# The last 32 tokens of a 16384-expert layer taken out of its dense products and gathered instead

## The reference, cut to what matters

```python
s = einsum('chpd,hpnd->chpn', (xb @ wq), keys)      # 8 heads, two halves, 128 keys each
sv, si = top_k(s, 16)                               # per half
cand, cidx = sums of the pairs, si0 * 128 + si1
top_s, sel = top_k(cand, 16); eidx = cidx[sel]      # 16 experts of 16384 per head and token
g = softmax(top_s)
act = gelu(einsum('chkd,cd->chk', u_tab[eidx], xb))
return einsum('chk,chkd->cd', g * act, v_tab[eidx])
```

## Time and profile before

| | |
|---|---|
| median of 3 runs | 3477.69 us (3469.15 to 3482.21) |
| profiled execution | 3476.73 us |
| its span, first to last instruction | 3474.9 us |
| mean granted TensorE clock | 0.942 |
| busy: PE, PEld | 3244.1 us (93%), 2621.2 us (75%) |
| busy: DVE, ACT, POOL | 1652.2 us (48%), 988.6 us (28%), 1323.9 us (38%) |
| first Gelu of the U pass, first and last matmul start of the V pass | 458.4, 1267.3 and 1963.6 us |

### The profile page before, as it was taken

The page is one execution under the profiler, slowest core; times in us unless marked ns, Lnnn a source line. Parts: engine busy times, 40 slices in busy tenths (PEclk is TensorE's granted clock), DMA queues, the critical chain, the costliest instruction groups (busy, mean ns, idle before and its releaser), DMA issues. The chain is left out here.

```text
span 3474.9 us, 40090 instructions
## 1 busy us (share of the span) xinstructions
PE 3244.1 (93%) x15270; PEld 2621.2 (75%) x15270; DVE 1652.2 (48%) x3968; ACT 988.6 (28%) x1534; POOL 1323.9 (38%) x637
## 2 busy tenths in 40 slices
PE   8696899999999999999999899899988899889998
PEld 7454687878787788888888578688867789768886
DVE  6764259989898623333333354433023055433311
ACT  2333233333333321111111212222212256422221
POOL 3101243434333345555555334344423145324442
PEclk9767899999999999999999999899989879989999
DMA  3001145546465665555555222222322000112231
GB/s 115 11 1 55 62 123 161 180 144 194 148 191 149 194 215 194 194 194 194 194 194 194 73 84 80 79 97 95 105 85 97 24 1 1 49 56 97 97 110 66
DMA packets 179844, 399.22 MB, mean 115 GB/s; under 512 B 13332, under 2 KB 80788, under 8 KB 175300
## 3 DMA queue, kind: packets, MB, share of 16 engines
q1 hardware_dynamic: 179508, 394.55, 35.3%
q10 hardware_dynamic: 144, 2.10, 0.2%
HBM read 327.39 MB, written 69.21 MB: 114 GB/s over the span
## 5 line engine op out<-in xcount | busy, mean ns | idle before, releaser
L239 POOL TENSOR_TENSOR peer_wt_lo<-peer_wt,peer_wt_hi 128x1024 fp32r<-128x1024 f32 x272 | 713.4, 2623 | 1095.8 <-ACT peer_wt_hi L232 1095.8
L239 POOL TENSOR_TENSOR ffn_w_lo<-ffn_w,ffn_w_hi 128x1024 fp32r<-128x1024 f32 (+1 forms) x120 | 314.6, 2622 | 453.7 <-ACT ffn_w_hi L232 453.7
L232 ACT ACTIVATE peer_wt_hi<-peer_wt 128x1024 fp32r<-128x1024 f32 x272 | 287.9, 1059 | 615.9 <-PE peer_psum L251 604.2
L249 PE MATMUL peer_psum<-xn_hi,peer_wt_hi 128*128 128x512 f32 x1088 | 435.3, 400 | 11.3 <-DVEq L447 11.1
L251 PE MATMUL peer_psum<-xn_hi,peer_wt_lo 128*128 128x512 f32 x1088 | 427.9, 393 | 0.0
L250 PE MATMUL peer_psum<-xn_lo,peer_wt_hi 128*128 128x512 f32 x1088 | 427.4, 393 | 0.0
L249 PE MATMUL peer_psum<-peer_w_hi,peer_wt_hi 128*128 128x512 f32 x1024 | 398.5, 389 | 0.7 <-ACT peer_act_out L1230 0.7
L250 PE MATMUL peer_psum<-peer_w_lo,peer_wt_hi 128*128 128x512 f32 x1024 | 398.3, 389 | 0.0
L251 PE MATMUL peer_psum<-peer_w_hi,peer_wt_lo 128*128 128x512 f32 x1024 | 398.3, 389 | 0.0
L1255 DVE TENSOR_SCALAR peer_first_hot<-peer_iota,idx,gate 128x128 f16<-128x128 f16 x1024 | 330.6, 362 | 0.0
L249 PE MATMUL ffn_psum<-ffn_hn_hi,ffn_w_hi 128*128 128x512 f32 x704 | 279.3, 397 | 20.2 <-DVEq L447 20.0
(11 more groups left out here) (354 smaller groups left out, 5860.3 us busy)
## 6 DMA issues: line engine op xcount, KB each, us to landing
peer_wt<-in_peer_uT SPq DMA_DIRECT2D x128, 512.0 KB, 4.3
peer_wt<-in_peer_v SPq DMA_DIRECT2D x128, 512.0 KB, 3.7
ffn_w<-in_f_w_gu SPq DMA_DIRECT2D x88, 512.0 KB, 3.6
peer_act<-peer_act_out SPq DMA_DIRECT2D x128, 256.0 KB, 4.6
peer_gate<-peer_gates_out SPq DMA_DIRECT2D x16, 2048.0 KB, 10.4
peer_gates<-peer_gate SPq DMA_DIRECT2D x32, 1024.0 KB, 5.0
peer_act_in<-peer_act SPq DMA_DIRECT2D x128, 256.0 KB, 2.6
ffn_w<-in_f_w_down SPq DMA_DIRECT2D x32, 704.0 KB, 4.0
```

The lines of the kernel that those rows point to most:

```text
L232: act.activation(self.hi[:, n % self.pairs, 0:c], self.buf[:, n % self.n, 0:c], ACT.Copy).then_inc(self.rounded, 1)
L239: pool.tensor_tensor(self.lo[:, n % self.pairs, 0:c], self.buf[:, n % self.n, 0:c], self.hi[:, n % self.pairs, 0:c].bitcast(F32), ALU.subt ...
L249: pe.matmul(out, w[0], x[0], start=start, stop=False)
```

## The change: what it does, and the diff

The last 32 tokens (`GT`) leave both dense passes, so that each dense matmul has 480 columns (`DTOK`) instead of 512; the stored activations and gates shrink with it. The gate blocks of these tokens (four of the 64, at tiles 110 to 113) are not made.

For the 32 tokens the expert rows are gathered. The 128 partitions hold four parts (`GRP`) of 32 tokens; each part takes 32 (`STEPS`) of a token's 128 experts. At step s POOL fetches by indirect DMA one row of 1024 floats for each partition (512 KB), into a ring of six (`ROWS`). For the U table DVE multiplies it with the token's row and sums it to one number (`first`); ACT applies Gelu to the 128x32 numbers; DVE makes the shares; for the V table DVE adds the row times its share to `acc` (`second_of`). `fold` adds the four parts on PE, in eight small matmuls beside the last V tile, which waits for `summed`.

The token rows are transposed on PE at tile 97 (`token_rows`, 16 float32 matmuls) and copied by ACT; at tile 100 SP spreads numbers, gates and rows over the partitions. Fetches 0 to 7 are issued by POOL between its last eight U splits, the others after them. DVE does the first eight steps ahead of the V pass, steps 8 to 31 at even tiles n = 0 to 46, and the V steps at even n = 52 to 114. POOL no longer splits the V tiles: DVE does (`split_to(dve, ...)`), between `L1359` and `L338` of the tile. A copy of the U table in row order is added to the inputs.

```diff
@@ -949,6 +955,12 @@
 HB = 8
 QB = 32
 QUAD = 4
+GT = 32
+DTOK = SEQ - GT
+GRP = P // GT
+STEPS = PH * TOPK // GRP
+ROWS = 6
+EARLY = 8

 def peer(kit, io):
...
+        share = at("shares", 48896, [P, STEPS])
+        fold = at("fold", 49152, [P, GT])
+        row = at("row_here", 50720, [P, D])
+
         shared = nc.sbuf_base
         room = st.sb("room", [P, 2 * CT * SEQ * 2])
         mix = Split(nc.alloc_sbuf_tensor_at("peer_mix_hi", [P, 2 * CT, SEQ], F32R, offset=shared),
                     nc.alloc_sbuf_tensor_at("peer_mix_lo", [P, 2 * CT, SEQ], F32R, offset=shared + 2 * CT * SEQ * 4))
+        G = nc.alloc_sbuf_tensor_at("peer_gathered", [P, ROWS, D], F32, offset=shared)
+        acc = nc.alloc_sbuf_tensor_at("peer_gather_sum", [P, D], F32, offset=shared + ROWS * D * 4)
...
         O1 = nc.alloc_sbuf_tensor_at("peer_first_hot", [P, 2, 2, HB, NK], F16, offset=io["mixT_at"] + 2 * HB * NK * 2)
         iota = st.sb("iota", [P, NK], F16)
...
@@ -1061,7 +1092,17 @@
 
         def block_at(c):
             j, b = divmod(c - TURN - 1, SLOTS)
-            return j * NB + b if 0 <= j < ST and b < NB else None
+            return j * NB + b if 0 <= j < ST and 0 <= b < NB and j * NB + b < DTOK // HB else None
+
+        def first_step(n):
+
+            return EARLY + n // 2 if n % 2 == 0 and EARLY + n // 2 < STEPS else None
+
+        SHARES = 2 * (STEPS - EARLY) + 3
+
+        def second_step(n):
+            s, odd = divmod(n - SHARES - 1, 2)
+            return s if not odd and 0 <= s < STEPS else None
 
         with nc.Block() as block:
...
-                        sp.dma_start(a_dram[n * P:(n + 1) * P, :], Ao[:, n % AS, :]).then_inc(a_stored[n % AS], 16)
+                        sp.dma_start(a_dram[n * P:(n + 1) * P, :], Ao[:, n % AS, 0:DTOK]).then_inc(a_stored[n % AS], 16)
+                    if c == SLOTS * (ST - 1) + TURN + 3:
+                        sp.wait_ge(experts_known, 2)
+                        for g in range(GRP):
+                            sp.dma_start(mine[g * GT:(g + 1) * GT, :, :],
+                                         chosen[P - GT:P, :, g * STEPS:(g + 1) * STEPS]).then_inc(spread, 16)
+                        sp.wait_ge(rows_copied, 1)
+                        for g in range(GRP):
+                            sp.dma_start(row[g * GT:(g + 1) * GT, :], rows[P - GT:P, :]).then_inc(spread, 16)
                     b = block_at(c - 1)
                     if b is not None and (b + 1) % (QB // HB) == 0:
                         s = b // (QB // HB)
...
@@ -1117,7 +1166,22 @@
 
             @block.gpsimd
             def _(pool):
-                lin.ring.split_all(pool)
+                def fetch(s, table):
+                    if s >= ROWS:
+                        pool.wait_ge(row_used, s - ROWS + 1)
+                    pool.indirect_dma_start(G[:, s % ROWS, :], None, table,
+                                            bass.IndirectOffsetOnAxis(mine[:, 0, s % STEPS:s % STEPS + 1], 0))\
+                        .then_inc(fetched[s % ROWS], 16)
+
+                lin.ring.split_to(pool, U0 + NK - EARLY)
+                pool.wait_ge(spread, 32 * GRP)
+                for i in range(2):
+                    pool.wait_ge(g_stored[i], 16 * len(range(i, DTOK // QB, 2)))
+                for s in range(EARLY):
+                    fetch(s, t["peer_u"])
+                    lin.ring.split_to(pool, U0 + NK - EARLY + s + 1)
+                for s in range(EARLY, 2 * STEPS):
+                    fetch(s, t["peer_u"] if s < STEPS else t["peer_v"])
 
             @block.tensor
...
+
+                def token_rows():
+
+                    last = slice(SEQ - P, SEQ)
+                    pe.wait_ge(s_copied, 4 * ST)
+                    for k in range(DT):
+                        to = ps[:, 4 + k // 4, (k % 4) * P:(k % 4 + 1) * P]
+                        pe.matmul(to, xn.hi[:, k, last].bitcast(F32), kit.ident[:, :], start=True, stop=False)
+                        mm = pe.matmul(to, xn.lo[:, k, last].bitcast(F32), kit.ident[:, :], start=False, stop=True)
+                    mm.then_inc(rows_turned, 1)
...
+                            token_rows()
                     if block_at(c) is not None:
                         gate_block(block_at(c))
...
-                        mm = product(pe, ps[:, c % 2, :], (whi[:, p], wlo[:, p]), xn.pair(slice(None), k),
-                                     k == 0, k == DT - 1)
+                        mm = product(pe, ps[:, c % 2, 0:DTOK], (whi[:, p], wlo[:, p]),
+                                     xn.pair(slice(None), k, slice(0, DTOK)), k == 0, k == DT - 1)
                     mm.then_inc(lin.done, 1)
 
                 pe.wait_ge(gelued, NK)
-                pe.wait_ge(gcopied, SEQ // 4)
+                pe.wait_ge(gcopied, DTOK // 4)
+                pe.wait_ge(rows_copied, 1)
                 pe.wait_ge(taken, 4 * ST)
                 for n in range(NK):
                     whi, wlo = lin.ring.take(pe, V0 + n)
                     pe.wait_ge(w_lo, n + 1)
+                    if n == NK - 1:
+                        pe.wait_ge(summed, 1)
                     for d in range(DT):
                         p = slice(d * P, (d + 1) * P)
-                        mm = product(pe, ps[:, d, :], (whi[:, p], wlo[:, p]), Ws.pair(slice(None), n % WS),
-                                     n == 0, n == NK - 1)
+                        mm = product(pe, ps[:, d, 0:DTOK], (whi[:, p], wlo[:, p]),
+                                     Ws.pair(slice(None), n % WS, slice(0, DTOK)), n == 0, n == NK - 1)
                         if n == NK - 1:
-                            mm.then_inc(odone, 1)
+                            pe.matmul(ps[:, d, DTOK:SEQ], acc[:, p], fold[:, :], start=True, stop=True).then_inc(odone, 1)
...
+                        act.activation(rows[:, :].rearrange("p (i n) -> p i n", i=2), ps[:, 4:6, :], ACT.Copy)\
+                            .then_inc(rows_copied, 1)
                     if c >= AS:
                         act.wait_ge(a_stored[c % AS], 16 * (c // AS))
                     act.wait_ge(lin.done, U0 + c + 1)
-                    act.activation(Ao[:, c % AS, :], ps[:, c % 2, :], ACT.Gelu).then_inc(gelued, 1)
+                    act.activation(Ao[:, c % AS, 0:DTOK], ps[:, c % 2, 0:DTOK], ACT.Gelu).then_inc(gelued, 1)
+                lin.ring.round_to(act, V0 + SHARES)
+                act.wait_ge(dotted, 1)
+                act.activation(dots[:, :], dots[:, :], ACT.Gelu).then_inc(dots_gelued, 1)
                 lin.ring.round_to(act, V0 + NK)
 
...
+                    if j == ST - 1:
+                        dve.scalar_tensor_tensor(out=chosen[:, 0, :], in0=three[:, 0, :], scalar=float(NK), in1=three[:, 1, :],
+                                                 op0=ALU.mult, op1=ALU.add).then_inc(experts_known, 1)
+                        dve.tensor_copy(chosen[:, 1, :].bitcast(F32), three[:, 2, :]).then_inc(experts_known, 1)
                     for b in range(NB):
-                        hots(j * NB + b)
+                        if j * NB + b < DTOK // HB:
+                            hots(j * NB + b)
+                dve.wait_ge(experts_known, 2)
+                dve.wait_ge(turned, ST)
+                own.link(dve.tensor_tensor(fold[:, :], kit.ident[:, 0:GT], kit.ident[:, GT:2 * GT], ALU.add))
+                for g in range(2, GRP):
+                    own.link(dve.tensor_tensor(fold[:, :], fold[:, :], kit.ident[:, g * GT:(g + 1) * GT], ALU.add))
+                dve.wait_ge(spread, 32 * GRP)
+
+                def first(s):
+
+                    dve.wait_ge(fetched[s % ROWS], 16 * (s // ROWS + 1))
+                    own.step(dve.scalar_tensor_tensor(out=G[:, s % ROWS, :], in0=G[:, s % ROWS, :], scalar=1.0, in1=row[:, :],
+                                                      op0=ALU.mult, op1=ALU.mult, accum_out=dots[:, s:s + 1]))
+                    own.wait()
+                    dve.nop().then_inc(row_used, 1)
+
+                def second_of(s):
+
+                    u = STEPS + s
+                    dve.wait_ge(fetched[u % ROWS], 16 * (u // ROWS + 1))
+                    own.wait()
+                    if s == 0:
+                        ins = dve.tensor_scalar(acc[:, :], G[:, u % ROWS, :], share[:, 0:1], None, ALU.mult)
+                    else:
+                        ins = dve.scalar_tensor_tensor(out=acc[:, :], in0=G[:, u % ROWS, :], scalar=share[:, s:s + 1],
+                                                       in1=acc[:, :], op0=ALU.mult, op1=ALU.add)
+                    own.step(ins)
+                    own.wait()
+                    dve.nop().then_inc(row_used, 1)
+
+                for s in range(EARLY):
+                    first(s)
 
                 for n in range(NK):
                     q, i = divmod(n, QUAD)
                     dve.wait_ge(a_in[n % AS], 16 * (n // AS + 1))
                     dve.wait_ge(g_in[q % 2], 16 * (q // 2 + 1))
-                    x = Wf[:, n % 2, :]
```

(23 more changed lines are left out.)

37 lines of the change are left out of this document (29 added, 8 removed).

## The result

The changed kernel takes **3422.9 us** (median of 4 runs, 3418.79 to 3427.71) against 3477.3 for the kernel before in the same runs: a ratio of 0.9847, 95% interval 0.9831 to 0.9863. That is 54.4 us less, where 69 were forecast. The profiled execution took 3419.84, with a span of 3418.1 against 3474.9.

The account below looks back on a forecast made before the run. PE was taken to bound V, DVE the gate tiles in U. Savings 41.0 + 19.2 + 3.0 + 7.6 - 0.2 - 1.6 = 69.0 us gave 3408; own range 3400 to 3417, 8 in 10 3398 to 3450.

Parts of the forecast that it names:

- small stalls where the fetches begin: Rival, 17%: slow POOL issues delay its last U splits, fetches land late at V's start; 3412 to 3440, say 3423.
- 480 columns in V: V pass, bound by PE: 3072 matmuls each 13.3 ns shorter, 41.0 us saved (38.1 to 43.5).
- Plain U tiles: U tiles without gate block or turn, bound by PE: 60 tiles x 0.32, 19.2 us saved.
- Turn and gate tiles of three groups: U pass, first three groups: DVE sets the pace from the turn, so only 1.0 us each, 3.0 together, saved.
- Tiles 110 to 113: U tiles that lose their gate blocks go from 7.02 to 5.12 us: 7.6 us saved.
- Token rows: Tile 97 in U: 16 float32 matmuls, 4.1 us, mostly covered by the first gate block's wait; 0.2 us lost.
- POOL: Issue of an indirect fetch taken as 1.5 us, fitting the 2.7 us between two U splits.
- Transfers: Fetches of 512 KB land in 3.7 us; traffic rises to some 250 GB/s, DMA share to 0.75: hidden.
- the slow fetches: Rival, 10%: fetches bound V, DVE waits for them and PE for DVE; 3590 at 14 us a fetch.
- Start of V: Fourth activation tile: load, store and reload move some 1.5 us ahead, so PE has no wait.
- The flat pitch: Rival, 4%: weight load plus gap set the 226.7 ns, so only the four gate blocks are saved; 3471.
- the outer gain: Rival, 3%: DVE does not bound the gate tiles, its held instruction being shorter; up to 13 us more, 3396.

Follow-up runs that it names:

- e1: Kernel before with the V pass's matmul width changed every eight tiles, from 512 down to 256 columns; 3419.79 us, one run.
- e2: Changed kernel without fetches, gather steps, token rows, folds and the wait for the sum; 3418.76 us, ratio 0.9837.
- e6: Changed kernel with DVE instead of POOL splitting the U tiles that fall beside gate blocks; 3390.32 us, ratio 0.9743.
- e3: Kernel before without its last four gate blocks, 512 columns everywhere, no gather; 3468.08 us, ratio 0.998.
- e4: Kernel before with DVE instead of POOL splitting the V tiles, nothing else; 3477.7 us, ratio 1.0009.
- e5: Changed kernel with 64 tokens gathered instead of 32, 448 columns, a gather step at nearly every V tile; 3363.05 us, ratio 0.9668.
- e10: e7 with SP's order changed where V starts: activations loaded back once their own tile is stored, no weight load ahead of the last stores; 3305.45 us.
- e7: Changed kernel with both 64 tokens gathered and the U tiles of the gate blocks split on DVE; 3310.15 us, ratio 0.9513.

## Why the prediction was right, and where it was off

The sign and the mechanism were right: PE bounds V and takes the narrower products, DVE bounds the gate tiles and takes nothing. The size was off: 14.6 of the 69 us are missing. 3422.9 lies outside the forecast's own range (3400 to 3417) and inside 3398 to 3450, which had been drawn that wide for the small stalls where the fetches begin. Of those only the 1.3 us at the start of V came; that the time fell on that rival's 3423 is luck. By the steps:

- **480 columns in V: the term that was mis-sized.** 41.0 us forecast at 13.3 ns a matmul; 10.0 ns were had, 3072 x 10.0 = 30.7. The step that was off is "32 columns fewer are 32 / 2.4 = 13.3 ns". It takes for granted that what stands beside the columns is the same at 480 as the 13.4 at 512; it is 16.7 (e1, e2). The forecast's other row hinted at that: 177 ns at 384 columns is 17 beside the columns. But it is a mean of three distances between starts rounded to 0.01 us, good to some 3 ns, and e1 has 173.4 at 384, so it could not tell 13.3 from 16.7. The lower bound of 12.4, drawn through these two widths, was too narrow: it says nothing of a third width within 3.3 ns.
- **Plain U tiles:** the same error, 60 x 0.24 = 14.4 us for 19.2.
- **Turn and gate tiles of three groups:** 3.0 forecast, 1.2 + 1.2 + 1.1 = 3.5 measured. Here counting from the block pace and not from PE's saving was worth 13 us of accuracy; e6 showed its cause.
- **Tiles 110 to 113:** 7.6 forecast, 28.1 to 20.8 = 7.3 measured (5.20 a tile); e3 confirms it alone, at 512 columns.
- **Token rows:** 0.2 lost forecast; tiles 97 to 109 went from 92.53 to 92.45: covered by the wait for the first block, as said. On PE they took 3.5 (1057.32 to 1060.81), for 4.1.
- **Folds:** 1.6 forecast, 1.7.
- **DVE in V:** 1.2 for the split and for a step with its drain 1.4 at most; measured 1.23, 1.22 + 0.08 and 1.28. Hidden (e4, e2).
- **POOL:** 1.5 an issue, measured 0.95, far under the 4 to 6 that the rival of small stalls needs. Its other ground was not put to the test: the early gather steps fell between POOL's splits (steps at 1196.45 and 1201.60, the split from 1198.11 to 1200.50). And the earlier trace rows does not bear on the rule that it is set beside, since the instruction held there reads one tensor from SBUF; one with two is L341 of the earlier trace rows, 2.80 us beside POOL's split instead of 0.69. The other way round, the issue that began beside a gather step at 1234.5 took POOL 1.99.
- **Transfers:** 0.75 and 250 GB/s forecast, 0.73 and 246. Landing took 4.2 to 7.9 us, 5.0 in the middle: the slow fetches fell, and e5 with twice as many still did not bring them about.
- **Start of V:** "no wait" was wrong by 1.3 us. The forecast had the fourth tile's activations some 1.5 us earlier than before; they came later, 14.1 us behind the first matmul of V (1258.02) where it had been 11.3 (1278.64). From there 2.8 us of DVE's work, 1.2 of it the split that now lies between, put the operand at 1260.8. SP's rows show both parts of the delay, in the kernel before and then in the kernel after:

```profile
1271.11 0.44 SPq L1093 DMA_DIRECT2D peer_act<-peer_act_out  x1
...
1275.96 3.73 SPq L1086 DMA_DIRECT2D peer_act_in<-peer_act  x4
```

```profile
1248.74 0.43 SPq L1134 DMA_DIRECT2D peer_act<-peer_act_out  x1
...
1255.36 3.66 SPq L1127 DMA_DIRECT2D peer_act_in<-peer_act  x4
```

SP loads nothing back before its last store has landed (the loop of waits that e10 takes out). That store goes out 4.8 us behind V's first matmul instead of 3.8, since a V weight load that waits for DVE's split stands ahead of it; and from there to the loads it takes 6.6 us instead of 4.9, beside the fetches. The wait of PE follows these two numbers through the runs: 2.6 and 4.3 without the gather, no wait (e2); 6.1 and 7.3 in e6, wait 3.0; 7.2 and 7.5 in e5, wait 6.5; 7.3 and 8.2 in e7, wait 7.6. With SP's order changed it is gone (e10).

Together in V: 10.3 from the pitch and 1.3 from the wait, 11.6 of the 39.4 net forecast missing (27.8 measured). In U: 4.8 from the pitch, 0.2 gained elsewhere, 25.0 for 29.6. That is 16.2 us on the two passes; the difference to the 14.6 between the medians lies in the rest and is within the noise.

The flat pitch fell (e1: 120.0 ns at 256 columns), and these runs show a slope of 0.42 ns a column. With it falls, for this kernel, the estimate of 0.13 ns a column worked out from the two spacings that the Trainium skill gives in TensorE: Matmul & The Clock Gate, Back-to-back issue gap. Shorter holds of DVE in the gate tiles, the outer gain, did not come either: 7.02 stayed.

## What to carry to other kernels

Before a time is worked out from columns over clock, take the pitch of exactly that form, width and start column, from a run: here what stands beside the columns was 13.4 ns at 512 and 16.7 at 480, and the difference was a quarter of the gain. A saving on one engine counts only in tiles where that engine sets the pace (16.3 us on paper became 3.5 in the gate tiles); look next at what holds the engine that does, since here POOL's split of 2.4 us held DVE for 2.15 and cost more than DVE's own 1.23. When a wait is taken away, measure the stretch and not the wait: in V of e10 the wait of 7.6 went and the pass grew by 2.5, since the pitch had changed.

## What the runs showed of the hardware that was not expected

- The pitch of a float32 product with 128x128 weights does not follow its columns evenly: 226.6 for 512 and 504 but 227.6 for 508, 223.4 for 496 and 500, 220.0 for 488, 216.7 for 480 (e1).
